# Decoder trunk step in split float32: sample turns in one pass, 96-row sample contraction, moved read-outs, pre-added squares, and an end shared by two engines

## The reference, cut to what matters

```python
def gated_linear_recurrence(q, k, v, log_f, s0):      # S_t = diag(exp(log_f_t)) S_{t-1} + k_t v_t^T
    ...
        att = jnp.einsum('bhtk,bhsk,bhtsk->bhts', qb, kb, decay)
        o = (jnp.einsum('bhts,bhsv->bhtv', att, vb)
             + jnp.einsum('bhtk,bhkv->bhtv', qb * jnp.exp(b), S))
        S_new = (jnp.exp(b_last[:, :, 0, :])[..., None] * S
                 + jnp.einsum('bhsk,bhsv->bhkv', kb * jnp.exp(b_last - b), vb))
def head_rms_norm(o, w):
    of = of * lax.rsqrt(jnp.mean(of * of, -1, keepdims=True) + EPS)
...
        o = head_rms_norm(o, norm_w) * jax.nn.silu(g)
        y = o @ w_out
        x = layer_norm(ALPHA * x + (1.0 + g1) * y, ln_w[l, 0], ln_b[l, 0])
```

## Time and profile before

| | |
|---|---|
| median of 3 runs | 3130.21 us (3129.75 to 3130.66) |
| profiled execution, its own time | 3132.57 us |
| its span | 3130.7 us |
| PE busy | 3055.7 us, 98% of the span |
| PE weight load busy | 2855.9 us, 91% |
| DVE busy | 1735.0 us, 55% |
| ACT busy | 1308.1 us, 42% |
| POOL busy | 292.2 us, 9% |
| HBM traffic | 218 GB/s over the span |

### The profile page before, as it was taken

One profiled execution on the slowest core, in us unless ns is written; L12 is line 12 of the kernel. 1 busy time (PEld: TensorE's weight loads), 2 busy tenths in 40 slices (PEclk: granted clock), 3 DMA queues, 4 the chain that ended last, 5 costly groups with the idle time before them and its releaser, 6 DMA issues.

```text
span 3130.7 us, 66319 instructions
## 1 busy us (share of the span) xinstructions
PE 3055.7 (98%) x26988; PEld 2855.9 (91%) x26988; DVE 1735.0 (55%) x2471; ACT 1308.1 (42%) x1702; POOL 292.2 (9%) x290
## 2 busy tenths in 40 slices
PE   7899999999999999999999899999999999999998
PEld 3689999989899999999998889987999999999998
DVE  2477766665744444444445666666574454454546
ACT  1355555553533333333333544544353343343433
POOL 0021111111300000000001301110130000000000
PEclk8999999999999999999999999999999999999999
DMA  9997888888777676776775775675545555555552
GB/s 377 323 309 248 258 256 268 269 289 271 269 243 234 207 258 210 235 250 193 250 238 181 249 230 167 199 235 189 157 135 167 164 167 168 163 168 164 167 166 74
DMA packets 541643, 685.68 MB, mean 219 GB/s; under 512 B 22225, under 2 KB 469257, under 8 KB 541065
## 3 DMA queue, kind: packets, MB, share of 16 engines
q1 hardware_dynamic: 484402, 625.43, 61.6%
q10 hardware_dynamic: 56960, 56.21, 5.5%
HBM read 650.88 MB, written 30.67 MB: 218 GB/s over the span
## 4 chain that ended last, share of the span: by engine, by line
PE 74%; DVE 3%; ACT 1%; DMA 0%; issue 0%; DVEq 0%; ACTq 0%
PE main L549 23%; PE main L551 22%; PE main L550 22%; PE bank L561 2%; PE bank L1143 1%; DVE z L2353 0%; PE bank L1128 0%; DVE z L2357 0%; PE bank L1114 0%; DVE a_lo L2387 0%; DVE w_lo L1854 0%; PE bank L691 0%; PE bank L1180 0%; DMA raw<-in_w_ada 0%; DMA out_new_gla_sample<-gl_s 0%; PE bank L579 0%
## 5 line engine op out<-in xcount | busy, mean ns | idle before, releaser
L1854 DVE TENSOR_TENSOR w_lo<-raw,w_hi 128x1024 fp32r<-128x1024 f32 x804 | 988.2, 1231 | 1189.6 <-ACT w_hi L1268 1186.0
L1268 ACT ACTIVATE w_hi<-raw 128x1024 fp32r<-128x1024 f32 x804 | 850.2, 1059 | 1508.7 <-PE main L551 1388.1
L549 PE MATMUL main<-a_hi,w_hi 128*128 128x288 f32 x4240 | 1282.3, 302 | 17.1 <-DVE a_lo L2387 13.8
L551 PE MATMUL main<-a_hi,w_lo 128*128 128x288 f32 x4240 | 1254.4, 296 | 0.0
L550 PE MATMUL main<-a_lo,w_hi 128*128 128x288 f32 x4240 | 1253.4, 296 | 0.0
L549 PEld LDWEIGHTS main<-a_hi,w_hi 128*128 128x128 f32 x4240 | 800.2, 189 | 58.8 <-issue 34.6
L550 PEld LDWEIGHTS main<-a_lo,w_hi 128*128 128x128 f32 x4240 | 799.7, 189 | 4.6 <-issue 1.9
L551 PEld LDWEIGHTS main<-a_hi,w_lo 128*128 128x128 f32 x4240 | 799.9, 189 | 0.0
L549 PE MATMUL main<-act_hi,w_hi 128*128 128x288 f32 x2048 | 606.3, 296 | 0.0
L551 PE MATMUL main<-act_hi,w_lo 128*128 128x288 f32 x2048 | 604.9, 295 | 0.0
L550 PE MATMUL main<-act_lo,w_hi 128*128 128x288 f32 x2048 | 601.9, 294 | 0.0
(11 more groups left out here) (319 smaller groups left out, 2032.0 us busy)
## 6 DMA issues: line engine op xcount, KB each, us to landing
raw<-in_w_ada SPq DMA_DIRECT2D x384, 512.0 KB, 6.7
raw<-in_w_up SPq DMA_DIRECT2D x256, 512.0 KB, 3.8
raw<-in_w_down SPq DMA_DIRECT2D x256, 512.0 KB, 3.5
raw<-in_hg_w_in SPq DMA_DIRECT2D x128, 512.0 KB, 6.5
raw<-in_gla_w_in SPq DMA_DIRECT2D x100, 512.0 KB, 3.9
raw<-in_hg_w_out SPq DMA_DIRECT2D x32, 512.0 KB, 7.7
gl_s<-in_state_gla ACTq DMA_DIRECT2D x32, 512.0 KB, 5.7
out_new_gla_sample<-gl_s ACTq DMA_DIRECT2D x32, 512.0 KB, 4.9
```

What stands on the lines that cost most here:

```text
L549: mm(out, hi, x_hi[:, kb, :], start=kb == 0, stop=False)
L551: last = mm(out, lo, x_hi[:, kb, :], start=False, stop=kb == KB - 1)
L1268: F(w_hi[:, st.split_slot(g)].rearrange("p k n -> p (k n)"), raw[:, slot, :], ACT.Copy).then_inc(hi_ready, 1)
L1854: V.tensor_tensor(w_lo[:, s].rearrange("p k n -> p (k n)"), raw[:, slot, :], w_hi[:, s].rearrange("p k n -> p (k n)").bitcast(F32), ALU.su ...
```

## The change

1. `turn_samples` is one transpose of 96 rows. Its source is a threefold copy of the 32 sample columns: for values ACT writes it (`hg_s3` in an enlarged `hg.sq`; `gl_sv`, on the memory of `gl_ksm`), for keys DVE writes it by one more multiply ahead of the key multiply (`hg_s3[:, 2:4]`, `gl.sk`).
2. `hg_out` and `gl_sample_out` contract over 96 rows; `atts` has 96 rows.
3. Read-outs 0 and 1 are in step 23, read-outs 2 and 3 in step 5; the loads of the next head's states on ACT go from steps 5 to 8 to steps 6 to 9.
4. DVE adds the four blocks of squares in step 10 (two adds), PE sums with one matmul in step 11, ACT makes `rstd` in step 11, and the scale goes from the start of DVE's step 10 work to the end of its step 12 (`gl_scale`).
5. At the end the last quarter's weight and bias are on DVE, PE transposes into eight banks, ACT copies eight pieces and DVE four, SP issues nine of the twelve stores and ACT three.

```diff
-        def turn_samples(bank, at, src, copies=3):
-
-            for j in range(copies):
-                last = mm(bank[32 * j:32 * j + 32, at:at + P], src, ident[:, :], start=True, stop=True,
-                          skip_group_check=True, tile_position=(0, 32 * j))
-            return last
+        def turn_samples(bank, at, src):
+
+            return turn(bank[0:96, at:at + P], src.rearrange("p c t -> p (c t)"), ident[:, :])
...
-            mm(b7[:, TP:T], hg["ts"][0:64, h, :].bitcast(F32), hg["atts"][:, h, :], start=False, stop=False,
+            mm(b7[:, TP:T], hg["ts"][:, h, :].bitcast(F32), hg["atts"][:, h, :], start=False, stop=False,
...
         def gl_sum(n):
-            pe.wait_ge(G["squared"], n + 1)
+            pe.wait_ge(G["sq_summed"], n + 1)
             pe.wait_ge(G["ss_read"], 8 * n + 8)
-            for v in range(4):
-                last = mm(b5[:, 0:T], ones[:, :], gl["v"][:, v, :], start=v == 0, stop=v == 3)
-            last.then_inc(G["summed"], 1)
+            mm(b5[:, 0:T], ones[:, :], gl["v"][:, 0, :], start=True, stop=True).then_inc(G["summed"], 1)
...
-                if s in (1, 4, 5):
-                    gl_read_out(pn, 1 if s == 1 else s - 2)
+                if s == 5:
+                    gl_read_out(pn, 2)
+                    gl_read_out(pn, 3)
...
-                if s == 10:
+                if s == 11:
                     gl_sum(pn)
...
                 elif s == 23:
                     gl_read_out(n, 0)
+                    gl_read_out(n, 1)
                     gl_sample(n, 0)
...
                     panel_done(HG, n, 11)
+                    F(hg_s3[:, 0:2], threefold(panel(HG, 2)[:, :, TP:T]), ACT.Copy)
...
-                if own and 5 <= s <= 8:
-                    gl_load(n, s - 5)
+                if own and 6 <= s <= 9:
+                    gl_load(n, s - 6)
...
-                if s == 10:
+                if s == 11:
                     head_rstd(G, pn + 1, b5, GLA_V)
...
             dve.wait_ge(H["kd_exp"], n + 1)
+            step(V.tensor_tensor(hg_s3[:, 2:4], threefold(hg["x"][:, 1, :, TP:T]), threefold(hg["k"][:, :, TP:T]), ALU.mult))
...
+        def gl_scale(pn):
+
+            dve.wait_ge(G["rstd_ready"], pn + 1)
+            o = o_buf[:, cols(4 * pn, 4), :]
+            step(V.tensor_tensor(o, o, rstd[:, :].unsqueeze(1).to_broadcast([P, 4, T]), ALU.mult))
+            for v in range(4):
+                o = o_buf[:, cols(4 * pn + v, 1), :].rearrange("p a t -> p (a t)")
+                last = V.scalar_tensor_tensor(out=o, in0=o, scalar=vec[:, cols(2 * KB + 4 * pn + v, 1)],
+                                              in1=gl["g"][:, v], op0=ALU.mult, op1=ALU.mult)
+            last.then_inc(G["o_ready"], 1)
...
                 if s == 10:
-                    dve.wait_ge(G["rstd_ready"], pn + 1)
-                    o = o_buf[:, cols(4 * pn, 4), :]
-                    step(V.tensor_tensor(o, o, rstd[:, :].unsqueeze(1).to_broadcast([P, 4, T]), ALU.mult))
-                    for v in range(4):
...
+                    dve.wait_ge(G["squared"], pn + 1)
+                    step(V.tensor_tensor(gl["v"][:, 0:2, :], gl["v"][:, 0:2, :], gl["v"][:, 2:4, :], ALU.add))
+                    V.tensor_tensor(gl["v"][:, 0, :], gl["v"][:, 0, :], gl["v"][:, 1, :], ALU.add).then_inc(G["sq_summed"], 1)
...
+            if prev and s == 12:
+                gl_scale(pn)
...
+Y_COPIES = {"A": [0, 1, 2, 3, 4, 5, 8, 11], "V": [6, 7, 9, 10]}
+Y_STORES = [0, 1, 2, 3, 4, 6, 7, 9, 10]
```

More of the change, by code:

```diff
@@ L213, in __init__ @@
         self.top = nc.sbuf_usable_end
+        self.start = {}
     def put(self, name, shape, dtype=F32, at=None):
@@ L382, in halves, with threefold @@
         return v[:, :, :, m:] if second else v[:, :, :, :m]
+    def threefold(v):
+        return v.unsqueeze(2).to_broadcast([P, v.shape[1], 3, TS])
     def last_of(v):
@@ L524, in _ @@
         mixer_stored(sp, G, GLA_HEADS * NB // 2, GLA_HEADS * 2)
+        for g in Y_STORES:
+            engine, count = y_copied(g)
+            sp.wait_ge(y_read[engine], count)
+            sp.dma_start(y_out(g), y_piece(g)).then_inc(y_stored, 16)
         sp.wait_ge(y_stored, 16 * 12)
@@ L748, in hg_sample_turn @@
             pe.wait_ge(mod_ready, 5 + pn)
-            for j, (src, h) in enumerate([("v", 0), ("v", 1), ("k", 0), ("k", 1)]):
-                src = hg["v"] if src == "v" else hg["x"][:, 1]
-                last = turn_samples(b7, j * P, src[:, h, TP:T])
+            for j in range(4):
+                last = turn_samples(b7, j * P, hg_s3[:, j])
             last.then_inc(H["s_turned"], 1)
@@ L796, in hg_sum @@
                 pe.wait_ge(H["rstd_ready"], 2 * pn + 1)
[L797 removed]
+            mm(b6[:, 0:T], ones[:, :], hg["sq"][:, 0:T], start=True, stop=True).then_inc(H["summed"], 1)
         def hg_prompt_state(pn):
@@ L1540, in hg_opening @@
             panel_done(HG, 0, HG_FIRST.index((2, 3)))
+            for h, bank in enumerate((b4, b5)):
+                F(hg_s3[:, h], bank[:, TP:T].unsqueeze(1).to_broadcast([P, 3, TS]), ACT.Copy)
             F(hg["v"][:, 0, :], b4[:, 0:T], ACT.Copy)
@@ L1771, in gl_step @@
                     panel_done(GLA, n, s - 1)
+                    F(gl_sv[:, 2 * j:2 * j + 2], threefold(panel(GLA, 2 + j)[:, :, TP:T]), ACT.Copy)
                     F(gl["v"][:, 2 * j:2 * j + 2, :], panel(GLA, 2 + j), ACT.Copy).then_inc(panel_read["A"], 1)
@@ L1827, in _, with y_affine @@
         layer_norm(3, None)
-        for c in range(4):
+        def y_affine(c):
             act.wait_ge(ln_scaled, 5 * 3 + c + 1)
@@ L1834, in _, with y_copy @@
             last.then_inc(y_ready, 1)
-        ys = A["y_prompt"][0, 0:P, :], A["y_prompt"][0, P:TP, :], A["y_sample"].rearrange("b t d -> (b t) d")
-        for c in range(4):
-            for i in range(3):
-                r = P if i < 2 else TS
-                act.wait_ge(y_read, 3 * c + i + 1)
-                act.dma_start(ys[i][:, c * 512:(c + 1) * 512], yout[0:r, i, c * 512:(c + 1) * 512]).then_inc(y_stored, 16)
+        def y_copy(first, last):
+            for g in Y_COPIES["A"][first:last]:
+                act.wait_ge(y_turned, g + 1)
+                F(y_piece(g), y_bank(g)[0:P if g % 3 < 2 else TS, :], ACT.Copy).then_inc(y_read["A"], 1)
+        y_affine(0)
+        y_copy(0, 1)
+        y_affine(1)
+        y_copy(1, 3)
+        y_affine(2)
+        y_copy(3, 7)
+        for g in (5, 8):
+            act.wait_ge(y_read["A"], y_copied(g)[1])
+            act.dma_start(y_out(g), y_piece(g)).then_inc(y_stored, 16)
+        y_copy(7, 8)
+        act.wait_ge(y_read["A"], 8)
+        act.dma_start(y_out(11), y_piece(11)).then_inc(y_stored, 16)
     @block.vector
@@ L2601, in _ @@
         layer_norm(3, None)
-        for g in range(12):
-            c, i = divmod(g, 3)
-            r = P if i < 2 else TS
+        dve.wait_ge(ln_scaled, 5 * 3 + 4)
+        for kb in range(12, 16):
+            last = V.tensor_scalar(z[:, kb, :], z[:, kb, :], lnv[:, 0, 1, 1, kb:kb + 1], lnv[:, 1, 1, 1, kb:kb + 1],
+                                   ALU.mult, ALU.add)
+        last.then_inc(y_last, 1)
+        for g in Y_COPIES["V"]:
             dve.wait_ge(y_turned, g + 1)
-            V.tensor_copy(yout[0:r, i, c * 512:(c + 1) * 512], main[0:r, g % 4, :]).then_inc(y_read, 1)
+            V.tensor_copy(y_piece(g), y_bank(g)[0:P if g % 3 < 2 else TS, :]).then_inc(y_read["V"], 1)
     @block.gpsimd
```

58 lines of the change are left out of this document (39 added, 19 removed).

## The result

The changed kernel takes 3136.14 us in the median of 16 runs (3129.61 to 3145.57), the kernel before 3130.68 (3128.29 to 3134.41, 16 runs). The ratio is 1.0018, with a 95% interval of 1.0012 to 1.0025: 5.5 us slower. I had forecast 3129.9, a gain of 0.3 us, and a chance of 0.48 for no change that can be told; the time is inside the stated range and inside the 0.2% that I called the same, but the difference is clear of zero and on the other side of it. The sum was off by 6.2 us. The profiled execution has a span of 3136.0 us, against 3130.7 before.

The account below looks back on a forecast made before the run. The prediction took PE, busy 98% of the span, to bound the kernel. Terms of 16.5 us gained and 16.2 lost left 0.3, taking the median from 3130.21 to 3129.9 us, with a range of 3114 to 3139.

Parts of the forecast that it names:

- The moved scale: GLA heads 1 to 3: the scale inside DVE's level chain stalls PE 4.3 us a head, -12.9 us.
- the sign: In PE's waits: a level's matmuls waiting on DVE's `gl_x` multiplies, three times, 3.6 to 4.8 us.
- The clock: Behind the PE stalls: half speed costs 1.65 us, in two of three heads, -3.3 us, bounds 0 and -5.
- Turns and 96 rows: HG and GLA samples on PE: turns +8.8 us, 96-row contraction +4.0, DVE's added multiply -0.5.
- The end: Last copies and stores: copies on two engines and eight banks end 1 to 3 us earlier, taken as +1.5.
- Squares: GLA heads: one sum matmul for four saves 4.35 us in three heads, last head -0.8; together +3.5.
- The read-outs: GLA heads: joining saves 1.6 us at best, waits for masks in steps 1 and 4 cost 2.4; -0.8 us.
- the one with POOL: Moved scale, GLA levels 2 and 3: POOL's sums hold it, 8.65 us a head lost, 3139.7 us; chance 0.20.

Follow-up runs that it names:

- experiment 1: Changed kernel with the scale of GLA heads 1 to 3 given one instruction a step in steps 14 to 18; 3122.63 us.
- experiment 5: Changed kernel with the read-outs in steps 23, 1, 4 and 5 and the state loads in steps 5 to 8, as before; 3128.11 us.
- experiment 6: Changed kernel with the scale of heads 1 to 3 one instruction a step in steps 14 to 18, and read-outs and loads as before; 3113.85 us.
- experiment 4: Changed kernel with squares, sum, `rstd` and scale as before; turns, 96 rows, read-out slots and end as changed; 3123.21 us.
- experiment 2: Kernel before with only the threefold copies, one-pass turns and 96-row contraction (points 1 and 2 of the change); 3118.17 us.
- experiment 7: Changed kernel with read-outs, squares and scale as before, leaving turns, 96 rows and the end; 3114.84 us.
- experiment 8: Experiment 6 with the last head's squares, sum, `rstd` and scale as before (four matmuls, no adds); 3113.45 us.
- 10: Experiment 6 with read-out 2 moved from step 4 to step 5 and the next head's state loads in steps 6 to 9; 3113.73 us.
- experiment 3: Kernel before with only point 4 of the change: pre-added squares, sum and `rstd` in step 11, scale at the end of step 12; 3146.17 us.

## Why the prediction missed, step by step

- **The moved scale** was right in mechanism and close in size. The stall was put at 4.3 us a head and measured at 3.8, the row of waits gives 11.4 for 12.9. PE waits for DVE's reads (`gl_near`), though, and not for the level multiplies that I had named as the sign. With the clock I had 16.2, and the trace has 11.4 + 5.7 = 17.1; taking the scale out of the chain gave 13.5 (changed to experiment 1) and 14.3 (experiment 5 to 6). That the chain's length came out right is in part luck. I had 8.28 + 4.34 = 12.62 us from the first level multiply to PE's start, and it is 12.76 (1989.85 to 2002.61). But the 8.28 were not all DVE's work: before, PE started 0.85 us behind the last read, after the change 0.14, so 0.71 us of them were PE's own. The scale is 0.39 us shorter at its new place, and POOL's operations cost the multiply and the split 1.24 us that they did not cost before. The three errors all but cancel.
- **The clock** fell at all three waits for the levels, not at two, and cost 1.7, 1.4 and 2.6 us, 5.7 against the 3.3 that I took, beyond my bound of 5. It fell at masks' waits too, of 1.72 to 2.71 us in experiment 4, for which I had counted nothing.
- **Turns and 96 rows**: 8.8 + 4.0 - 0.5 = 12.3 forecast, 12.1 measured. A turn of 96 rows costs 0.09 us instead of 0.133 (0.07 in the pair of key turns), the 96-row product saves 0.19 where I took 0.2. PE's one wait for the decayed keys of HG is 1.1 us in experiment 2 as before, so the trace shows no cost of DVE's added multiply; the 2.7 us of waits for loads were not in the sum. That the two totals agree so closely is in part luck.
- **The end**: 1.5 forecast, 3.3 measured with a wide interval, and 1.4 by the two profiles of before and after. The size stays open.
- **Squares**: 3.5 forecast. In the best version they are worth 1.0 us (3114.84 to 3113.85, within the scatter), so the term was put too high by about 2.5: the sum saves 1.45 a head as said, but 0.4 a head is still lost to the levels, and the last head waits 2.0 us for the adds.
- **The read-outs are the step that failed.** I wrote -0.8 with bounds of -3 and +1.6; the slots cost 8.0 us (changed to experiment 5), 8.4 (experiment 4 to 7) and 8.8 (experiment 1 to 6). I had priced the mask from one row in which it was 0.71 us early, and took its time as fixed. But the mask stands on DVE behind a state update, and that update waits for the store of two states before (the text on the kernel before says that the stores free the mask's buffer; they free the update's). A store lands 4.5 us after its issue in the median of experiment 6, and the two stores above held DVE until 8.1 and 10.0 us after it; the DMA share was 1.05 or more in the windows behind such waits. Where the mask is late, PE loses the whole read-out's cover, some 1 us, and half speed follows behind part of the waits, 1.7 us each. The term had no room for either. About half of the 8 us is read-out 1's move. That read-out 2's move costs nothing alone, and that the sum of the parts (4.4 and at most 2) is below 8, stays open: two moves together may cost more than each.

The errors add up: 8.0 for 0.8 at the read-outs and 2.5 less for the squares is 9.7 us, against 2 to 3 us less for the scale with its clock (13.5 to 14.3 for 16.2) and 0 to 2 us more from the end. That leaves 5 to 8 us, and 6.2 was measured.

Of the rivals, the one with POOL did not decide, though what it names was there. It said that the scale lay where POOL was at rest and would lie where POOL forms its sums. Before, two of the scale's five operations already stood beside POOL (1.19 and 0.92 us instead of 0.51), and after the change two do (0.75 and 0.99), so the scale took 3.95 us and not more than 4.34. The first level multiplies and the split lost 1.24 us to POOL instead. The rule of the Trainium skill, "SBUF — State Buffer", section "Who interferes with whom", says that of a DVE operation with two SBUF inputs and a GpSimd operation that reads SBUF the one that starts second waits until the first is through. The trace agrees: the multiply of 1.21 us and the scale's two start under an operation of POOL (of 1989.89, 1995.80 and 1996.93) and each ends 0.31 to 0.33 us behind its end.

The best version that came out is experiment 8's (or that of 6 or 10, which can't be told from it): 3113.45 us, 0.53% faster than before.

## What to carry to other kernels

When an operation is moved on an engine of 55% load, don't ask whether there is room, but which chain it now stands in: the same five instructions made the bottleneck engine wait 3.8 us a head inside the chain that it waits for, and 0.4 where they were given out one by one behind it. Work that stands ahead of a wait is a cover; before joining two pieces to save a change of shape of some tenths, look up what waits right behind the piece that leaves, over all its repetitions and not in one, above all where a DMA is the last link. Price a mask or buffer by the latest of its rows.

## What was not expected of the hardware

- Half speed came behind waits of less than 2 us: in experiment 4 two of 1.72 us had a stretch of 3.41 us at 0.50 behind them, as the waits of 3.8 us did. In the same kernel a wait of 2.76 us had none, so the length of the wait alone does not tell.
- Waits of the same length did not cost the same: of three of 3.8 us in the changed kernel two had 3.41 us at 0.50 and the third 6.83; in experiment 3 all three had 6.83.
- The changed kernel scatters more than the kernel before: 16.0 us from the lowest to the highest of 16 runs, against 6.1. The experiments with long waits for masks or levels scatter too (8.7 to 10.2 us over 7 or 11 runs), but so does experiment 7 (7.0 over 5 runs), which has few. What scatters is not shown.
